# Shifting two operand buffers of a two-block transformer kernel by 32 bytes in each partition

## What is computed

```python
def first_block(...):
    for l in range(DEPTH):
        h = rms_norm(x, g_mix[l])
        proj = h @ w_in[l]
...
        merged = (gates[:, :, 0] * y_a + gates[:, :, 1] * y_b
                  + gates[:, :, 2] * y_c + gates[:, :, 3] * y_d)
        x = x + merged @ w_merge[l]

        h2 = rms_norm(x, g_ffn[l])
        gt = causal_dwconv(h2 @ w_ffn_gate[l], ffn_conv_w[l])
        x = x + (jax.nn.silu(gt) * (h2 @ w_ffn_up[l])) @ w_ffn_down[l]
    return x
```

## The kernel before

| buffer | start before | modulo 64 | start of its first element after | modulo 64 |
|---|---|---|---|---|
| whi | 41,088 | 0 | 41,088 | 0 |
| wlo | 57,472 | 0 | 57,472 | 0 |
| hhi | 74,304 | 0 | 74,336 | 32 |
| hlo | 82,496 | 0 | 83,040 | 32 |
| fhi | 130,112 | 0 | 131,168 | 32 |
| flo | 138,304 | 0 | 139,872 | 32 |
| fin | 183,360 | 0 | 184,384 | 0 |
| xn | 109,600 | 32 | 110,624 | 32 |
| w1 | 146,496 | 0 | 148,544 | 0 |
| w2 | 130,112 | 0 | 131,136 | 0 |

## Time and profile before

### The profile page before, as it was taken

The page is one execution under the profiler, slowest core; times in us unless marked ns, Lnnn a source line. Parts: engine busy times, 40 slices in busy tenths (PEclk is TensorE's granted clock), DMA queues, the critical chain, the costliest instruction groups (busy, mean ns, idle before and its releaser), DMA issues. The chain is left out here.

```text
span 1369.2 us, 26498 instructions
## 1 busy us (share of the span) xinstructions
PE 1345.0 (98%) x10828; PEld 1265.4 (92%) x10828; DVE 1040.0 (76%) x1781; ACT 750.9 (55%) x1157; POOL 46.3 (3%) x48
## 2 busy tenths in 40 slices
PE   8999999999999999999999999999999999999998
PEld 8899999998999989899999999999989899888996
DVE  6999898677766666999897767766778746777565
ACT  6544656556444455544557545544558546576363
POOL 0000000000000000000000000000000110001100
PEclk9999999999999999999999999999999999999999
DMA  8565444564665465645364555555553324353231
GB/s 289 177 207 178 131 154 160 180 215 155 197 202 185 139 230 163 215 155 185 97 204 159 187 187 172 198 185 191 178 186 124 120 64 137 100 174 109 78 102 69
DMA packets 108992, 223.77 MB, mean 163 GB/s; under 512 B 6180, under 2 KB 17700, under 8 KB 108872
## 3 DMA queue, kind: packets, MB, share of 16 engines
q1 hardware_dynamic: 106736, 219.12, 48.2%
q10 hardware_dynamic: 2136, 2.96, 0.7%
HBM read 221.01 MB, written 1.06 MB: 162 GB/s over the span
## 5 line engine op out<-in xcount | busy, mean ns | idle before, releaser
L1755 DVE TENSOR_TENSOR wlo<-ring,whi 128x1024 fp32r<-128x1024 f32 (+3 forms) x430 | 498.1, 1180 | 182.7 <-ACT whi L1173 152.7
L1173 ACT ACTIVATE whi<-ring 128x1024 fp32r<-128x1024 f32 (+3 forms) x430 | 433.2, 1026 | 361.8 <-PE bank L499 228.7
L499 PE MATMUL bank<-hhi,whi 128*128 128x256 f32 x2016 | 278.8, 280 | 6.0 <-ACT sgb L1431 3.9
L508 PE MATMUL bank<-hhi,wlo 128*128 128x256 f32 x2016 | 280.3, 281 | 0.0
L499 PE MATMUL bank<-hlo,whi 128*128 128x256 f32 x2016 | 275.3, 278 | 0.0
L499 PEld LDWEIGHTS bank<-hhi,whi 128*128 128x128 f32 x2016 | 253.1, 189 | 9.5 <-ACT sgb L1431 4.3
L508 PEld LDWEIGHTS bank<-hhi,wlo 128*128 128x128 f32 x2016 | 252.6, 189 | 3.7 <-issue 2.6
L499 PEld LDWEIGHTS bank<-hlo,whi 128*128 128x128 f32 x2016 | 251.6, 189 | 0.0
L469 PE MATMUL bank<-w 64*64 64x64 f32 (+5 forms) x1376 | 101.7, 249 | 1.5 <-DMA w<-in_flip 0.9
L1935 DVE SCALAR_TENSOR_TENSOR w<-w,par 128x256 f32<-128x256 f32 x240 | 98.0, 478 | 0.0
L521 PE MATMUL bank<-whi,hhi 128*128 128x512 f32 (+2 forms) x256 | 96.6, 379 | 0.0
(11 more groups left out here) (309 smaller groups left out, 1535.5 us busy)
## 6 DMA issues: line engine op xcount, KB each, us to landing
ring<-in_w_in SPq DMA_DIRECT2D x100, 1024.0 KB, 5.1
ring<-in_w_ffn_down SPq DMA_DIRECT2D x22, 1024.0 KB, 5.1
ring<-in_w_ffn_gate SPq DMA_DIRECT2D x20, 1024.0 KB, 5.1
ring<-in_w_ffn_up SPq DMA_DIRECT2D x20, 1024.0 KB, 5.1
ring<-in_w_merge SPq DMA_DIRECT2D x8, 1024.0 KB, 5.1
ring<-in_w_out SPq DMA_DIRECT2D x8, 1024.0 KB, 5.0
ring<-in_w_oc SPq DMA_DIRECT2D x4, 1024.0 KB, 5.3
ring<-in_w_od SPq DMA_DIRECT2D x4, 1024.0 KB, 5.2
```

Source lines behind the costliest of these rows:

```text
L499: done = e.matmul(o, wh[:, k, cols(u)], s_[:, k0 + k, :], stop=False, skip_group_check=True, start=opens and k == 0 and s_ is sh and u % 2 ...
L508: done = e.matmul(o, wl[:, k, cols(u)], sh[:, k0 + k, :], start=False, stop=closes, skip_group_check=True)
L1173: e.activation(part_of(whi, j), part_raw(j), ACT.Copy).then_inc(*up("hi.a"))
L1755: e.tensor_tensor(part_of(wlo, j), part_raw(j), part_of(whi, j), ALU.subtract).then_inc(*up("lo.v"))
```

## The change

hhi, hlo, fhi and flo are each declared as one row of 8 x 256 + 128 elements in a partition, and a helper, aside, takes the 8 x 256 elements that begin at element 8, which is 32 bytes in, and views them as 8 slices. F[q] is then slices 4q to 4q + 3, as it was. Nothing else is edited. The four buffers grow by 512 bytes a partition each, so that what is declared behind them moves by 1,024 or 2,048 bytes. No instruction is added, taken away or put elsewhere on any engine: the instructions of the two programs are the same ones in the same order, apart from their line numbers, which are three higher behind the helper.

```diff
--- before.py
+++ after.py
@@ -197,8 +197,11 @@
         cs = sb("cs", [P, 2, 48])
         posi = sb("posi", [P, 2], I32)
         posf = sb("posf", [P, 2])
-        hhi = sb("hhi", [P, 8, S], F32R)
-        hlo = sb("hlo", [P, 8, S], F32R)
+        def aside(ap):
+            return ap[:, 8:8 + 8 * S].rearrange("p (c s) -> p c s", s=S)
+
+        hhi = aside(sb("hhi", [P, 8 * S + 128], F32R))
+        hlo = aside(sb("hlo", [P, 8 * S + 128], F32R))
         cst = sb("cst", [P, NCN])
         par = sb("par", [P, L * NPL])
         onesb = sb("onesb", [P, 128])
@@ -213,8 +216,8 @@
         first = ExitStack()
-        fhi = first.enter_context(nc.sbuf_tensor("fhi", [P, 2, 4, S], F32R))
-        flo = first.enter_context(nc.sbuf_tensor("flo", [P, 2, 4, S], F32R))
+        fhi = aside(first.enter_context(nc.sbuf_tensor("fhi", [P, 8 * S + 128], F32R)))
+        flo = aside(first.enter_context(nc.sbuf_tensor("flo", [P, 8 * S + 128], F32R)))
         w1 = first.enter_context(nc.sbuf_tensor("w1", [P, 18568], F32))
         first.close()
@@ -276,7 +279,7 @@
         fy, fsg = A1.rearrange("p (c s) -> p c s", c=4), B1.rearrange("p (c s) -> p c s", c=4)
-        F = [(fhi[:, q], flo[:, q]) for q in range(2)]
+        F = [(fhi[:, 4 * q:4 * q + 4], flo[:, 4 * q:4 * q + 4]) for q in range(2)]
```

## The result

The changed kernel takes 1397.02 us (1396.59 and 1397.45), the kernel before 1373.95: 1.0165 times the time, with a 95% interval of 1.0115 to 1.0214. It is slower, by 23 us, and the interval reaches over the 2% that I took as the bound of what can be told. The forecast was 1371.

The account below looks back on a forecast made before the run. TensorE's own matmul pace was taken as the bound (98% busy). Between nothing and 7 us, 3 us gained was taken: 1369.2 - 3 = 1366.2 us of span, plus 4.8 us around it, 1371 us; range 1345 to 1400.

Parts of the forecast that it names:

- Cost of the writing lines at nothing: Lines L1210, L1812, L1480 and L2255 writing the four buffers: no cost taken, at most 2 us reaching TensorE.
- Term 1: 256-column matmuls, 6,821 intervals: 9.5 us gained if all at 113.3 ns, 21 us lost if all at 117.8.
- the long step: Slower of two steady 256-column matmul paces in the trace: 117.8 ns against 113.3, held by some 30% of intervals.
- The sign that I had named for the slow side: TensorE timeline: stretches at 0.98 us or more per eight matmuls, or the FFN's long stretch at 0.94.
- Term 2: 512-column matmuls, 1,200 reading moved buffers: 3.6 us gained if all at 226 ns, 3.6 lost if all at 232.
- Term 3: Unexplained floor under both forms' paces: 40 us if all gone, but taken at nothing, as going with the moving stream.
- Rival B: Floor goes too, streaming collides with the load when both start in the same place: 1321 to 1335 us; chance 0.12.
- The 324-wide matmul: Rows alternating 0 and 16 modulo 64: 148.3 against 147.3 ns, 0.7% shorter, read as place acting on the steps.
- The 8-wide loads: L1091, weights 8 columns wide: 113 ns at either distance, taken as evidence that the floor is not the load's.
- Rival C: Chans matmuls at L499, L508 slower off a 64-byte place: 1395 to 1426 us; chance 0.18, 0.10 beyond 27 us.
- Rival A: All large matmuls at their fastest pace, coincidence at 0 modulo 64 causing the long step: 1361 us; chance 0.18.
- Rival D: Change does nothing, since paces are set by phases in time and not by place: 1374 us; chance 0.12.

Follow-up runs that it names:

- sweep2: Separate program, against the first such program: 512 columns at 16 distances, 256 at six entries, and 8-wide weights; the 8-wide stood at 113.3 to 113.7 ns at ten distances.
- weights32: Against the changed kernel: only whi and wlo begin 32 bytes in, the four activation buffers back at 0; 1.0151 times the kernel before.
- plus64: Against the changed kernel: the four activation buffers begin 64 bytes in instead of 32; 1.0180 times the kernel before.
- both16: Against the kernel before: whi, wlo, hhi, hlo, fhi and flo all begin 16 bytes in; 0.9932 times it, 1365.67 us against 1375.58.
- plus16: Against the changed kernel: the four activation buffers begin 16 bytes in instead of 32; 1.0185 times the kernel before.

## Why the prediction was right or wrong

- **What bounds the kernel: right.** TensorE's pace is the end. The waits did not grow in sum, no other engine has more work, and 25.9 us of changed intervals are 25.6 us of span.
- **Cost of the writing lines at nothing: right.** 401 and 343 ns as before.
- **Term 1, choice wrong and the bound short.** "If all on the long step: 6,821 x (117.8 - 114.7) = 21 us lost" is near what happened, but that all intervals grew by 21.0 us is in part luck: the pace went past the long step, to 118.29 ns, 24.4 us, and some 3 us came back, mostly because the clock no longer fell. I chose a gain. The sign that I had named for the slow side did come: the feed-forward's long stretch stands at 0.95 us per eight.
- **Term 2, a little short at its end.** I bounded it by the 232 ns seen among single matmuls, 3.6 us; the mean went to 233.0, 4.9 us.
- **Term 3, right.** No block of any sweep, and no kernel, has a pace below 113.3 and 226.7 ns, with loads of 8 columns either. That the rest over the columns goes with the moving stream fits this but is not shown, since no run is without a load. Rival B is out.
- **The step that failed** is "By that share terms 1 and 2 would be 1,055 us x 0.7% = 7 us gained ... I take 3 us gained". The 324-wide matmul compares distances 64 and 80 modulo 256, of the toks form. I read it as 0 against 16 modulo 64 and carried it to 192 against 224 of another form. What the runs showed in its place: both new distances have a slower pace than the old ones, which cost 24.4 us on the one form and 4.9 on the other, where I had 3 us gained. The map has no slope that could be carried: from 96 to 112 to 128 bytes it goes 119.9, 113.3, 120.0. It would not even have held at 512 columns, where 64 and 80 are 228.9 and 231.1, the other sign.
- **The 8-wide loads** The earlier trace rows were taken as "either distance" without effect. They do show what I used them for, that the floor stays. But they read a sixteenth of the weights' columns, and sweep2 shows that this takes the place's effect away at most distances. A witness from which the cause was removed could not speak for a full load.
- **The rivals.** Rival C, "Price at the long step 21 us: 1395", comes nearest the time, and I gave that half 0.08. Its mechanism, a stream off its 64-byte place, is wrong: the 256-column streams of weights32 and plus64 begin on a 64-byte place and are slow, and both16 has every stream off one and is the fastest. Rival A fell with its reason, since sharing a place modulo 64 is not what makes the long step. Rival D, no effect, is out.
- **The Trainium skill**, "TensorE: Matmul & The Clock Gate", section "Step-by-step: what each phase is for", says that the load of the next weights takes no read bandwidth from the running matmul. Here the same stream beside the same load takes 113.3 to 120.0 ns by place alone, and mostly 113.3 when the load is 8 columns. The measurement decides: beside a full load of float32r weights the stream runs up to 6% slower than at its best place.
- **What lies around the span** was taken as 4.8 us. In the changed kernel's profiled execution it is 1396.59 - 1394.8 = 1.8 us; most of the rest was the difference between two runs of before. By the span, the forecast of 1366.2 missed 1394.8 by 28.6 us.

The cause in one sentence: the kernel before stood by luck at the pair of distances 192 and 64, which are among the best for their forms, and the 32 bytes moved both to 224 and 32, which are not. Sharing a place modulo 64 was not what kept it fast: plus64 shares it and is slow.

## What to carry to other kernels

When TensorE is the bound and its weights change with every matmul, print for each form the start of the moving operand less that of the stationary one, modulo 256, and where both stand modulo 64, and hold the pace per matmul from the timeline beside it. Starts moved with no instruction changed cost up to 1.9% here (plus16) and gave 0.7% (both16), and a buffer added or resized ahead of the operands can move them, so compare kernels at like places. A place is tried in a small sweep of all 16-byte steps rather than reasoned out from one of them, and for each form by itself, since the best place of one (distance 0 of 512 columns) can be the worst of the other.

## What the runs showed of the hardware that I had not expected

- The pace of back-to-back float32r matmuls with a full load beside each depends on the relative place of the two operands in a partition, with a period of 256 bytes: 113.3 to 120.0 ns for 256 columns, 226.7 to 236.9 for 512.
- At one distance it depends on the common place too: at distance 112, 113.3 to 114.1 ns with the stationary operand at 0 or 32 and 120.0 at 16 or 48.
- Distances that are no multiple of 16 can be worse still: 4 bytes gave 122.8 to 123.3 ns, 8 bytes 126.7 at two of three entries.
- Some pairs have two stable paces and keep the one that they entered: 113.3 or 117.8 at distance 192, after nothing but another number of small matmuls ahead.
- A slower pace can be partly hidden by the clock: the kernel before has two stretches at the 1.2 GHz level (0.51 from 168.0 to 171.3 us), each after a wait of 2.0 us for ScalarE, and the slower changed kernel, with waits of at most 1.3 us there, has neither.
- How the memory is laid out that makes it so, no run here shows.
